# A fused two-block kernel: the layers' low halves on VectorE alone, the bias table loaded and masked later, head norms loaded once

## The chip, the cores and the metric

The kernel runs on one NeuronCore of a Trainium2 chip. Its engines are TensorE (PE), VectorE (DVE), ScalarE (ACT), GpSimd (POOL) and SyncE (SP), which only issues loads here. The metric is the device time of one execution in microseconds, as the median of several runs. Lower is better.

## The reference

The input is 256 tokens of width 1024 in float32. A first block (adaptive norm, two attentions, a mixture of 32 experts) is followed by a second block of two layers. Only the second block's layers are touched by the change. Cut to what matters:

```python
def second_block(x, ...):
    for l in range(DEPTH_2):                                  # 2 layers
        h = rmsnorm(x, norm_mix_pre[l])
        proj = jnp.einsum('bsd,de->bse', h, w_in[l])          # 1024 -> 5888
        qa, ka, va, pu, qc, kc, vc, gl = jnp.split(proj, splits, axis=-1)
        ya = global_axial_attention(qa, ka, va, qk_norm_q[l], qk_norm_k[l])
        yb = pool_mixer(pu, w_pool[l], pool_scale[l])
        yc = neighbourhood_attention(qc, kc, vc, rpb[l])
        ...                                                   # gates, branches, w_out
        x = x + rmsnorm(mix, norm_mix_post[l])
        h = rmsnorm(x, norm_ffn_pre[l])
        f = conv_gated_mlp(h, w_up[l], conv_w[l], conv_b[l], w_down[l])
        x = x + rmsnorm(f, norm_ffn_post[l])
    return x

def global_axial_attention(q, k, v, gq, gk):
    q = rmsnorm(q.reshape(B, S, A_HEADS, HEAD_DIM), gq)       # 8 heads of 64, one gain row gq
    k = rmsnorm(k.reshape(B, S, A_KV_HEADS, HEAD_DIM), gk)    # 2 heads
    q = rope_2d(q, row, col) * (HEAD_DIM ** -0.5)
    k = rope_2d(k, row, col)
    ...                                                       # softmax(q k) v

def neighbourhood_attention(q, k, v, rpb):
    ...                                                       # keys of a 16 column window
    bias = rpb[:, dr[None, :, None], dc[:, None, :]]          # s + bias, softmax, times v
```

## The kernel before

**Units and halves.** In a layer the weights come in 66 units of 1 MB (128 partitions x 2048 float32), which SP loads in a fixed order into a ring of three slots (`RING_L`). The first 23 units are `w_in`: 0 and 1 give q of attention a, 2 gives its k and v, 3 and 4 the pooling input, 5 and 6 q of attention c, 7 to 10 its k and v, 11 to 22 the gates. A product with such a unit is made in three passes of TensorE over rounded halves: ScalarE copies the unit to a rounded high half (`take_high`, L1730), then the low half, unit minus high half, is made, and TensorE multiplies high by high, low by high and high by low (L739, 48 matmuls a unit). There are two pairs of halves, so the high half of unit u waits until TensorE is done with unit u - 2. SP loads unit u when the low half of unit u - 3 is made.

**Who makes the low halves.** VectorE does it in `take_low` (L1417) with one subtraction 128x2048, for all units but 5, 6, 7 and 8, which `POOL_LOW` gives to GpSimd (L1918). `low_half_done` tells waiting engines which semaphore counts for a unit, `low_done` or `low_done_pool`.

**The start of a layer.** VectorE normalises x, TensorE turns it, then units 0 to 6 (`EARLY` = 7) are multiplied. Pooling products follow (L1048 and after), then transposes of the rotated q and k (L1062, L1067), scores of attention a, units 7 to 10, its values, scores of attention c, units 11 to 22. VectorE's order is written out by hand: low halves 1 to 4, then norm and rotation of q and k (L1448 to L1478), which ends in `rope_ready`, then the scores' evacuation with row maximum (`keep_scores`, L1132), the scaling by the sum (`normalise`, L1146), low halves 9 to 12 and the scores of c, for which `bias_masked` must be there.

**GpSimd's part of a layer.** It waits for x (`layer_in`), issues six loads on its own queue (L1908, L1909): the head norm of q, repeated for 8 heads, and of k, for 2 heads (into `gqk`), the pooling weights, the two post norm rows (into `gpost2`, all on 128 partitions), and the bias table of attention c (`tables`, 2 MB, from `neighbours`). When the table is in, it adds the window mask in one operation of 4096 columns (L1913) and sets `bias_masked`. Then it makes its four low halves, and much later the gated products of the MLP (L1925 to L1927).

## Time and profile before

| | us |
|---|---|
| median of 3 runs | 2227.37 |
| lowest, highest | 2223.24, 2229.26 |
| the profiled execution, its own time | 2221.66 |
| its span in the trace | 2220.0 |
| TensorE busy | 2024.0 (91%) |
| VectorE busy | 817.1 |
| ScalarE busy | 706.2 |
| GpSimd busy | 296.8 |
| first layer of the second block, from its first weight load | 1263.6 |
| second layer, first load of GpSimd's | 1741.6 |

The profile is of one execution. The chain of work that ended last is followed back from the last instruction, at each step to what released it; a piece named "issue" is time in which the engine waited for nothing that the profile shows, and a piece of a line is the part of that instruction that lies on the chain. In the timeline a row is a start, a duration, the engine, the line, what is written from what is read, and in brackets how long the engine stood idle before it and what ended that. Ends of matmuls are modelled: neighbouring ones overlap by 0.1 to 0.2 us in the rows. q1 is the queue of SP's loads, q0 that of GpSimd's; both run on the same 16 DMA engines.

### The profile page before, as it was taken

To read this page: it belongs to the slowest core of one execution; us is meant where nothing else is said; L and a number is where in the kernel's file an instruction comes from. 1 tells how busy PE (TensorE), PEld (TensorE's weight loads), DVE (VectorE), ACT (ScalarE), POOL (GpSimd) and SP (SyncE) were. 2 spreads that over 40 slices of the span, in tenths; PEclk is the share of its full clock that TensorE was granted. 3 is DMA by queue.
4 is the path that set the end of the run, shared out by engine and by line. 5 is a ranking of instruction groups with operands and counts; after the bars stand their busy time and mean duration, and the time that the engine had idled before them with its cause. 6 is when DMAs were issued, how large, how long until landed. Compare 5 with 4: busy or idle time off the path is not lost.

```text
span 2220.0 us, 30251 instructions
## 1 busy us (share of the span) xinstructions
PE 2024.0 (91%) x11629; PEld 1316.4 (59%) x11630; DVE 817.1 (37%) x1341; ACT 706.2 (32%) x1092; POOL 296.8 (13%) x221
## 2 busy tenths in 40 slices
PE   5998699999999999999999689997999679997998
PEld 2785333333333333333333278986998679987996
DVE  2443411211111111112111266425775475245763
ACT  2434111111111111111111335514553346415553
POOL 3040100000000010001000131000341140000440
PEclk7899699999999999999999889998999889998999
DMA  9776699998996999799999864434555733443553
GB/s 355 153 279 265 258 416 418 418 417 344 398 418 283 418 418 417 316 418 417 417 416 417 297 183 130 149 117 152 171 190 171 180 117 118 149 171 129 181 184 114
DMA packets 203889, 609.45 MB, mean 275 GB/s; under 512 B 10946, under 2 KB 115542, under 8 KB 167408
## 3 DMA queue, kind: packets, MB, share of 16 engines
q1 hardware_dynamic: 197600, 585.40, 68.8%
q0 software_dynamic: 5872, 21.87, 4.4%
q8 instruction: 61, 1.00, 0.2%
q10 hardware_dynamic: 328, 0.95, 0.1%
q14 instruction: 28, 0.23, 0.0%
HBM read 605.03 MB, written 9.24 MB: 277 GB/s over the span
## 4 chain that ended last, share of the span: by engine, by line
PE 66%; DMA 12%; DVE 7%; issue 6%; SPq 5%; ACT 4%; DVEq 0%; ACTq 0%
PE bank L739 29%; PE bank L996 15%; PE bank L1025 9%; DMA ring<-in_w_gate_up 7%; DMA ring<-in_w_in 4%; PE bank L1089 3%; PE bank L956 2%; SPq L620 2%; SPq L623 2%; DVE split L1417 1%; ACT probs L1572 1%; PE bank L969 1%; PE bank L989 1%; DMA ring<-in_w_ada 1%; ACT split L1730 1%
## 5 line engine op out<-in xcount | busy, mean ns | idle before, releaser
L996 PE MATMUL bank<-ring,qkv 128*64 128x512 f32 x2240 | 497.3, 597 | 13.6 <-DMA ring<-in_w_gate_up 13.6
L739 PE MATMUL bank<-hT_hi,split 128*128 128x256 f32 x2432 | 442.0, 285 | 7.2 <-DVE hT_lo L1425 4.0
L739 PEld LDWEIGHTS bank<-hT_hi,split 128*128 128x128 f32 x2432 | 381.5, 193 | 10.4 <-issue 6.4
L1417 DVE TENSOR_TENSOR split<-ring,split 128x2048 fp32r<-128x2048 f32 x112 | 275.0, 2456 | 262.5 <-ACT split L1730 262.5
L1730 ACT ACTIVATE split<-ring 128x2048 fp32r<-128x2048 f32 x120 | 229.6, 1913 | 422.7 <-PE bank L739 318.9
L996 PEld LDWEIGHTS bank<-ring,qkv 128*64 128x64 f32 x2240 | 155.4, 137 | 338.5 <-issue 294.2
L739 PE MATMUL bank<-hT_lo,split 128*128 128x256 f32 x1216 | 345.3, 284 | 0.0
L1025 PE MATMUL bank<-ring,qkv 128*64 128x512 f32 x1120 | 255.8, 598 | 25.7 <-ACT qkv L1691 22.7
L739 PEld LDWEIGHTS bank<-hT_lo,split 128*128 128x128 f32 x1216 | 234.7, 193 | 0.0
L1395 DVE SCALAR_TENSOR_TENSOR out_halves<-bank,probs,out_halves 64x512 fp32r<-64x512 f32 x70 | 52.5, 750 | 395.5 <-ACT out_halves L1713 395.0
L1385 DVE TENSOR_SCALAR qkv<-bank 128x512 f32<-128x512 f32 x35 | 24.2, 692 | 421.2 <-PE bank L996 421.2
L1701 ACT ACTIVATE qkv<-qkv 128x512 f32<-128x512 f32 x35 | 22.1, 631 | 482.0 <-DVE qkv L1385 482.0
L1025 PEld LDWEIGHTS bank<-ring,qkv 128*64 128x64 f32 x1120 | 85.2, 136 | 148.8 <-issue 116.8
L1889 POOL TENSOR_TENSOR bias_halves<-qkv,small 4x512 fp32r<-4x512 f32 x32 | 41.4, 1294 | 906.1 <-DMA qkv<-in_b_gate_up 906.1
L739 PE MATMUL bank<-split,hT_hi 128*128 128x256 f32 (+1 forms) x576 | 131.2, 323 | 22.2 <-DVE split L1417 17.9
L739 PEld LDWEIGHTS bank<-split,hT_hi 128*128 128x128 f32 x576 | 101.9, 206 | 29.7 <-DVE split L1417 19.7
L1925 POOL TENSOR_TENSOR gated_hi<-probs 128x512 fp32r<-128x512 f32 x22 | 40.8, 1853 | 583.7 <-ACT probs L1801 583.7
L739 PE MATMUL bank<-split,gated_hi 128*128 128x512 f32 x352 | 109.3, 390 | 2.0 <-DVE split L1417 2.0
L739 PE MATMUL bank<-split,hT_lo 128*128 128x256 f32 (+1 forms) x288 | 92.5, 321 | 0.0
L1695 ACT ACTIVATE qkv<-bank 128x512 f32<-128x512 f32 x36 | 21.5, 597 | 215.2 <-PE bank L962 215.2
L1089 PE MATMUL bank<-mixT,ring 128*128 128x256 f32 x384 | 83.4, 380 | 1.5 <-ACT mixT L1564 1.5
L1089 PEld LDWEIGHTS bank<-mixT,ring 128*128 128x128 f32 x384 | 72.8, 190 | 12.2 <-issue 2.4
(282 smaller groups left out, 2375.8 us busy)
## 6 DMA issues: line engine op xcount, KB each, us to landing
ring<-in_w_gate_up SPq DMA_DIRECT2D x256, 1024.0 KB, 16.9
ring<-in_w_down SPq DMA_DIRECT2D x150, 1024.0 KB, 15.6
ring<-in_w_in SPq DMA_DIRECT2D x58, 1024.0 KB, 5.5
ring<-in_w_up SPq DMA_DIRECT2D x44, 1024.0 KB, 5.1
ring<-in_w_ada SPq DMA_DIRECT2D x24, 1024.0 KB, 9.8
ring<-in_w_out SPq DMA_DIRECT2D x12, 1024.0 KB, 4.9
ring<-in_w_branch SPq DMA_DIRECT2D x12, 1024.0 KB, 5.1
neighbours<-rpb_copies POOLq DMA_DIRECT2D x32, 128.0 KB, 9.3
```

Source lines behind the costliest of these rows:

```text
L620: sp.dma_start(unit_at(u), wgu[:, u, :]).then_inc(landed_moe[u], 16)
L623: sp.dma_start(rows_unit(u), wdn[:, 2 * v:2 * v + 2, :]).then_inc(landed_moe[u], 16)
L739: last = pe.matmul(out, a[a_half], b[b_half], start=start and i == 0, stop=stop and i == 2)
L956: last = pe.matmul(rows_bank[CAP * j:CAP * j + CAP, :], sel[:, tt, :], htok[:, tt, 512 * j:512 * j + 512], start=(tt == 0), stop=(tt == TT ...
L996: last = pe.matmul(hidden[q][CAP * j:CAP * j + CAP, :], xgT[:, k % 4, k // 4, :], unit_at(k)[:, c:c + 512], start=False, stop=(k == KC - 1))
L1025: last = pe.matmul(rows_bank[CAP * half:CAP * half + CAP, :], actT[:, f % 4, f // 4, :], rows_unit(KC + v)[:, c, 512 * half:512 * half + 5 ...
L1089: last = pe.matmul(bs[i][:, c * T:c * T + T], wv[:, k, n0:n0 + P], mixT[:, 4 * (u // 2) + k, :], start=(k == 0), stop=(k == 3))
L1395: last = dve.scalar_tensor_tensor(out=y_halves[there, half, :], in0=banks[6][here, :], scalar=slot_gate[here, :], in1=y_halves[here, half, ...
L1417: dve.tensor_tensor(low, unit_at(u % RING_L), high.bitcast(F32), ALU.subtract).then_inc(low_done, 1)
L1730: act.activation(split_halves(u)[0], unit_at(u % RING_L), ACT.Copy).then_inc(high_done, 1)
L1889: pool.tensor_tensor(bias_halves[0].rearrange("r (a t) -> r a t", t=T), brows.rearrange("r (a t) -> r a t", t=T), zeros[96:100, :].unsquee ...
L1925: own(pool.tensor_tensor(high, value, gate, ALU.mult))
```

## The change

The change has four edits, all in the layers' loop.

- `POOL_LOW` and its semaphore go. VectorE makes all low halves; those of units 5 to 8 are put at three places of its order: 5 behind the mean squares of q and k, 6 behind the product with the head norms, 7 and 8 behind `rope_ready`.
- The head norms are loaded once for all heads: `gqk` has 2 x 64 columns in place of 640, and the product with it is two operations that read the row once for each head, in place of one.
- GpSimd issues the loads of the table and then of the two post norm rows only when TensorE is done with the seventh unit. The post norms have a semaphore of their own, `gpost_in`, for which VectorE waits before the first post norm.
- The mask is added in sixteen operations of 256 columns, one for each token tile and head.

```diff
-PARAMS_IN = 5
+PARAMS_IN = 3
+GPOST_IN = 2
...
-POOL_LOW = [5, 6, 7, 8]
-DVE_LOW = [u for u in SPLIT if u not in POOL_LOW]
...
-        gqk = scratch(8448, 640)
+        gqk = scratch(8448, 2 * DH).rearrange("p (i d) -> p i d", i=2)
...
-            mine, done = (POOL_LOW, low_done_pool) if u in POOL_LOW else (DVE_LOW, low_done)
-            return done, l * len(mine) + (mine.index(u) + 1)
+            return low_done, l * len(SPLIT) + (SPLIT.index(u) + 1)
...
                     .then_inc(qk_means, 1)
+                take_low(5)
                 dve.wait_ge(roots, seen(roots))
...
-                own(dve.tensor_tensor(qk, qk, gqk.unsqueeze(1).broadcast_to([P, TT, n_heads * DH]), ALU.mult))
+                for i, (a, n) in enumerate(((0, HEADS), (MIX, A_KV))):
+                    part = qk[:, :, a:a + n * DH].rearrange("p t (h d) -> p t h d", d=DH)
+                    last = dve.tensor_tensor(part, part, gqk[:, i, :].unsqueeze(1).unsqueeze(1).broadcast_to(
+                        [P, TT, n, DH]), ALU.mult)
+                own(last)
+                take_low(6)
...
                 last.then_inc(rope_ready, 1)
+                take_low(7, 8)
                 keep_scores("a", lambda tt, h: zeros)
...
+                dve.wait_ge(gpost_in, 16 * GPOST_IN * (l + 1))
                 post_norm([f"mix{j}" for j in range(4)], gpost2[0], x_mid)
...
-                loads = [(gqk[:, 0:MIX].rearrange("p (h d) -> p h d", d=DH), over_heads(qk_q, HEADS)),
-                         (gqk[:, MIX:].rearrange("p (h d) -> p h d", d=DH), over_heads(qk_k, A_KV)),
-                         (wpool, w_pool[one].rearrange("l g c d -> (l c) g d")),
-                         (gpost2[0], norm_mix_post[one].rearrange("l d -> (l d)").partition_broadcast(P)),
-                         (gpost2[1], norm_ffn_post[one].rearrange("l d -> (l d)").partition_broadcast(P))]
+                loads = [(gqk[:, 0, :], qk_q[one].rearrange("l d -> (l d)").partition_broadcast(P)),
+                         (gqk[:, 1, :], qk_k[one].rearrange("l d -> (l d)").partition_broadcast(P)),
+                         (wpool, w_pool[one].rearrange("l g c d -> (l c) g d"))]
...
+                pool.wait_ge(unit_done_l, l * N_UNITS + (RING_L + EARLY))
+                posts = [(gpost2[0], norm_mix_post[one].rearrange("l d -> (l d)").partition_broadcast(P)),
+                         (gpost2[1], norm_ffn_post[one].rearrange("l d -> (l d)").partition_broadcast(P))]
                 pool.dma_start(tables.rearrange("p t h k -> p (t h k)"),
                                neighbours[one].rearrange("l p t h k -> (l p) (t h k)")).then_inc(bias_l_in, 16)
+                for to, source in posts:
+                    pool.dma_start(to, source).then_inc(gpost_in, 16)
                 pool.wait_ge(bias_l_in, 16 * (l + 1))
-                groups = tables.rearrange("p t h (r c) -> p (t h r) c", c=GRID_W)
-                pool.tensor_tensor(groups, groups, const("window").unsqueeze(1).broadcast_to(
-                    [P, TT * HEADS * GRID_H, GRID_W]), ALU.add).then_inc(bias_masked, 1)
-                for u in POOL_LOW:
-                    pool.wait_ge(high_done, l * len(SPLIT) + (SPLIT.index(u) + 1))
-                    high, low = split_halves(u)
-                    pool.tensor_tensor(low, unit_at(u % RING_L), high.bitcast(F32), ALU.subtract).then_inc(low_done_pool, 1)
+                for tt in range(TT):
+                    for h in range(HEADS):
+                        piece = tables[:, tt, h, :].rearrange("p (r c) -> p r c", c=GRID_W)
+                        last = pool.tensor_tensor(piece, piece, const("window").unsqueeze(1).broadcast_to(
+                            [P, GRID_H, GRID_W]), ALU.add)
+                last.then_inc(bias_masked, 1)
```

VectorE between the projection of k and v and the first scores, in program order, before (L1417 is a low half; those of the units 2 to 4 stand ahead, the norm and rotation behind):

```order
L1417 TENSOR_TENSOR split<-ring,split 128x2048 [waits high_done]
L1448 TENSOR_TENSOR ring<-qkv 128x1280 [waits bank_free_l6]
L1449 TENSOR_REDUCE qkms<-ring 128x20 [waits dve_own]
L1452 RECIPROCAL qkr<-qkms 128x20 [waits roots]
L1455 TENSOR_TENSOR qkv<-qkv,qkr 128x1280 [waits dve_own]
L1457 TENSOR_TENSOR qkv<-qkv,ring 128x1280 [waits params_in]
L1465 TENSOR_TENSOR probs<-qkv,consts 128x640 [waits dve_own]
L1474 TENSOR_TENSOR qkv<-probs 128x2x512 [waits dve_own]
L1478 TENSOR_TENSOR probs<-probs 128x2x64 x4
```

The same place of the changed kernel, where the low half is L1416:

```order
L1447 TENSOR_TENSOR ring<-qkv 128x1280 [waits bank_free_l6]
L1448 TENSOR_REDUCE qkms<-ring 128x20 [waits dve_own]
L1416 TENSOR_TENSOR split<-ring,split 128x2048 [waits high_done]
L1452 RECIPROCAL qkr<-qkms 128x20 [waits roots]
L1459 TENSOR_TENSOR qkv<-qkv,ring 128x2x512 [waits params_in]
L1459 TENSOR_TENSOR qkv<-qkv,ring 128x2x128
L1416 TENSOR_TENSOR split<-ring,split 128x2048 [waits high_done]
L1470 TENSOR_TENSOR probs<-qkv,consts 128x640
L1483 TENSOR_TENSOR probs<-probs 128x2x64 x4
L1416 TENSOR_TENSOR split<-ring,split 128x2048 [waits high_done]
L1416 TENSOR_TENSOR split<-ring,split 128x2048 [waits high_done]
```

Low halves 5 and 6 now stand inside norm and rotation, 7 and 8 between it and the scores.

GpSimd from the start of a layer to the gated products, before:

```order
L1908 ISA [waits layer_in]
L1908 DMA ring<-in_qk_norm_q 128x8x64
L1908 DMA ring<-in_qk_norm_k 128x2x64
L1908 DMA ring<-in_w_pool 128x4x128
L1908 DMA side<-in_norm_mix_post 128x1024
L1908 DMA side<-in_norm_ffn_post 128x1024
L1909 DMA ring<-neighbours 128x4096
L1913 TENSOR_TENSOR ring<-ring,consts 128x4096 [waits bias_l_in]
L1918 TENSOR_TENSOR split<-ring,split 128x2048 [waits high_done]
L1925 TENSOR_TENSOR gated_hi<-probs 128x512 [waits gelu_ready]
```

And in the changed kernel:

```order
L1910 ISA [waits layer_in]
L1910 DMA ring<-in_qk_norm_q 128x64
L1910 DMA ring<-in_qk_norm_k 128x64
L1910 DMA ring<-in_w_pool 128x4x128
L1916 ISA [waits unit_done_l]
L1916 DMA ring<-neighbours 128x4096
L1919 DMA side<-in_norm_mix_post 128x1024
L1919 DMA side<-in_norm_ffn_post 128x1024
L1924 TENSOR_TENSOR ring<-ring,consts 128x256 [waits bias_l_in]
L1924 TENSOR_TENSOR ring<-ring,consts 128x256 x15
L1933 TENSOR_TENSOR gated_hi<-probs 128x512 [waits gelu_ready]
```

The table and the post norms moved behind the wait for `unit_done_l`, the table ahead of them, and the four low halves (L1918, of which one row stands above) are gone.

## Rows read from the trace of the kernel before

**Rows 1.** The page: busy time of each engine, share of the span, instructions.

```profile
PE 2024.0 (91%) x11629; PEld 1316.4 (59%) x11630; DVE 817.1 (37%) x1341; ACT 706.2 (32%) x1092; POOL 296.8 (13%) x221
```

**Rows 2.** A window over the first layer's start: stretch, length, busy engines, PEclk, DMA, GB/s.

```profile
1264.00:1344.00 80.00, 56.12 (x379) 53.99 (x379) 55.23 (x43) 32.29 (x48) 34.94 (x11) 0.83 0.71 192
```

**Rows 3.** The chain that ended last, first layer: start, length on the chain, what.

```profile
1283.94 21.30 DMA ring<-in_w_in
...
1307.89 6.22 issue
1314.10 5.86 DVE ring L1448
```

**Rows 4.** The same chain, start of the second layer.

```profile
1745.75 26.89 DMA ring<-in_w_in
...
1774.68 7.16 DVE split L1417
...
1798.40 5.70 DVE qkv L1457
```

**Rows 5.** Timeline of ScalarE: high halves that TensorE released.

```profile
1335.83 1.91 ACT L1730 ACTIVATE split<-ring 128x2048 fp32r<-128x2048 f32 x1 [5.00 <-PE bank L739]
...
1417.42 1.91 ACT L1730 ACTIVATE split<-ring 128x2048 fp32r<-128x2048 f32 x1 [3.12 <-PE bank L739]
...
1423.18 1.91 ACT L1730 ACTIVATE split<-ring 128x2048 fp32r<-128x2048 f32 x1 [3.12 <-PE bank L739]
```

**Rows 6.** Timeline of TensorE: its idle times in both layers' starts.

```profile
1302.26 0.39 PE L739 MATMUL bank<-split,hT_hi 128*128 128x256 f32 x1 [2.35 <-DVE split L1417]
...
1314.23 0.58 PE L739 MATMUL bank<-split,hT_hi 128*128 128x256 f32 x1 [4.45 <-DVE split L1417]
...
1343.61 1.97 PE L1062 MATMUL bank<-consts,qkv 128*128 128x128 f32 x8 [2.63 <-DVE probs L1478]
...
1781.88 0.58 PE L739 MATMUL bank<-split,hT_hi 128*128 128x256 f32 x1 [9.62 <-DVE split L1417]
...
1818.14 1.97 PE L1062 MATMUL bank<-consts,qkv 128*128 128x128 f32 x8 [4.14 <-DVE probs L1478]
```

**Rows 7.** DMA queue q0 in 1276:1282 and 1298:1300: packets, MB, share of engines.

```profile
q0 software_dynamic: 32, 0.13, 105.8%
...
q0 software_dynamic: 27, 0.41, 48.4%
```

**Rows 8.** Timeline of GpSimd: mask, two low halves, a product of 512 columns.

```profile
1303.06 8.96 POOL L1913 TENSOR_TENSOR ring<-ring,consts 128x4096 f32<-128x4096 f32 x1 [27.45 <-DMA ring<-neighbours]
...
1324.67 5.05 POOL L1918 TENSOR_TENSOR split<-ring,split 128x2048 fp32r<-128x2048 f32 x1 [6.07 <-ACT split L1730]
...
1570.27 1.30 POOL L1926 TENSOR_TENSOR probs<-probs 128x512 f32<-128x512 f32 x1
...
1792.32 4.59 POOL L1918 TENSOR_TENSOR split<-ring,split 128x2048 fp32r<-128x2048 f32 x1 [12.64 <-ACT split L1730]
```

**Rows 9.** Timeline of VectorE: low half, rotation, reciprocal, normalisations, scores of c.

```profile
1299.91 2.29 DVE L1417 TENSOR_TENSOR split<-ring,split 128x2048 fp32r<-128x2048 f32 x1 [7.24 <-ACT split L1730]
...
1325.31 5.09 DVE L1465 TENSOR_TENSOR probs<-qkv,consts 128x640 f32<-128x640 f32 x1
...
1335.55 0.81 DVE L1465 TENSOR_TENSOR probs<-qkv,consts 128x640 f32<-128x640 f32 x1
...
1355.38 2.19 DVE L1146 TENSOR_SCALAR probs<-probs,small 128x256 f32<-128x256 f32 x8
...
1359.33 2.19 DVE L1146 TENSOR_SCALAR probs<-probs,small 128x256 f32<-128x256 f32 x8
1361.44 2.28 DVE L1417 TENSOR_TENSOR split<-ring,split 128x2048 fp32r<-128x2048 f32 x1
...
1383.80 0.42 DVE L1132 CUSTOM_DVE_ANT_0 probs<-bank,ring 128x256 f32<-128x256 f32 x1 [3.96 <-issue]
...
1792.95 0.28 DVE L1452 RECIPROCAL qkr<-qkms 128x20 f32<-128x20 f32 x1 [6.00 <-ACT qkms L1758]
```

More of the change, by code:

```diff
@@ L486, in build @@
         landed_l = [sem(f"landed_l{s}") for s in range(RING_L)]
-        high_done, low_done, low_done_pool, hT_high = (sem(n) for n in ("high_done", "low_done", "low_done_pool", "hT_high"))
+        high_done, low_done, hT_high = (sem(n) for n in ("high_done", "low_done", "hT_high"))
         unit_done, tile_done = sem("unit_done"), sem("tile_done")
@@ L504, in build @@
         y_ready, moe_done = sem("y_ready"), sem("moe_done")
-        layer_in, params_in, bias_l_in, bias_masked = sem("layer_in"), sem("params_in"), sem("bias_l_in"), sem("bias_masked")
+        layer_in, params_in, gpost_in = sem("layer_in"), sem("params_in"), sem("gpost_in")
+        bias_l_in, bias_masked = sem("bias_l_in"), sem("bias_masked")
         qk_means, rope_ready, branch_ready, gated_ready = sem("qk_means"), sem("rope_ready"), sem("branch_ready"), sem("gated_ready")
@@ L1896, in _ @@
                 pool.wait_ge(layer_in, TT * l + TT)
-                def over_heads(a, n):
-                    return a[one].rearrange("l d -> (l d)").unsqueeze(0).broadcast_to([n, DH]).partition_broadcast(P)
-                loads = [(gqk[:, 0:MIX].rearrange("p (h d) -> p h d", d=DH), over_heads(qk_q, HEADS)),
-                         (gqk[:, MIX:].rearrange("p (h d) -> p h d", d=DH), over_heads(qk_k, A_KV)),
-                         (wpool, w_pool[one].rearrange("l g c d -> (l c) g d")),
-                         (gpost2[0], norm_mix_post[one].rearrange("l d -> (l d)").partition_broadcast(P)),
-                         (gpost2[1], norm_ffn_post[one].rearrange("l d -> (l d)").partition_broadcast(P))]
+                loads = [(gqk[:, 0, :], qk_q[one].rearrange("l d -> (l d)").partition_broadcast(P)),
+                         (gqk[:, 1, :], qk_k[one].rearrange("l d -> (l d)").partition_broadcast(P)),
+                         (wpool, w_pool[one].rearrange("l g c d -> (l c) g d"))]
                 assert len(loads) == PARAMS_IN
@@ L1908, in _ @@
                     pool.dma_start(to, source).then_inc(params_in, 16)
+                pool.wait_ge(unit_done_l, l * N_UNITS + (RING_L + EARLY))
+                posts = [(gpost2[0], norm_mix_post[one].rearrange("l d -> (l d)").partition_broadcast(P)),
+                         (gpost2[1], norm_ffn_post[one].rearrange("l d -> (l d)").partition_broadcast(P))]
+                assert len(posts) == GPOST_IN
                 pool.dma_start(tables.rearrange("p t h k -> p (t h k)"),
                                neighbours[one].rearrange("l p t h k -> (l p) (t h k)")).then_inc(bias_l_in, 16)
+                for to, source in posts:
+                    pool.dma_start(to, source).then_inc(gpost_in, 16)
                 pool.wait_ge(bias_l_in, 16 * (l + 1))
-                groups = tables.rearrange("p t h (r c) -> p (t h r) c", c=GRID_W)
-                pool.tensor_tensor(groups, groups, const("window").unsqueeze(1).broadcast_to(
-                    [P, TT * HEADS * GRID_H, GRID_W]), ALU.add).then_inc(bias_masked, 1)
-                for u in POOL_LOW:
-                    pool.wait_ge(high_done, l * len(SPLIT) + (SPLIT.index(u) + 1))
-                    high, low = split_halves(u)
-                    pool.tensor_tensor(low, unit_at(u % RING_L), high.bitcast(F32), ALU.subtract).then_inc(low_done_pool, 1)
+                for tt in range(TT):
[4 more added lines that the diff above has]
+                last.then_inc(bias_masked, 1)
                 own.loop(l, 2 * UPAIRS)
```

## The prediction, made before the changed kernel ran

> **What bounds the kernel now.** I first looked for the stage that the diff touches, since the mean over the span says little: TensorE is busy 91% of it and GpSimd 13% [rows 1]. The code that changes is the start of the two layers of the second block, at about 1263 us and 1735 us, up to the first attention. There I read the chain that ended last. It should run through matmuls if TensorE were the bound. It doesn't: in the first layer it runs through a weight load that takes 21.30 us to land, then through VectorE operations that last about 4.4 us too long [rows 3]; in the second through a load of 26.89 us and VectorE operations of 7.16 and 5.70 us [rows 4].
>
> Then I looked at TensorE's own timeline for what this costs. In a steady stretch one weight unit takes 5.76 us (ScalarE's high halves of two neighbouring units start at 1417.42 and 1423.18, each ending its wait for TensorE) [rows 5]. In the first layer TensorE idles 2.35 and 4.45 us between units and 2.63 us before the transposes of q and k; in the second 9.62 us in one piece and 4.14 us before the transposes [rows 6]. The clock falls with such gaps too: its mean granted share in this stretch of the first layer is 0.83 [rows 2].
>
> Why is the load late? GpSimd's queue q0 moved 32 packets, 0.13 MB, in the 6 us from 1276 and held the 16 engines 105.8% of that time: 6 x 16 x 1.058 / 32 = 3.2 us for a 4 KB packet. Behind the head norms, two microseconds of the table's stretch moved 27 packets with 0.41 MB at 48.4%, 0.57 us each, most of 16 KB [rows 7]. The slow packets are made of 256 byte pieces, the head norm repeated for each head. The two head norm loads are 128 x (8 + 2) x 256 bytes = 320 KB, 80 packets, 80 x 3.2 / 16 = 16 us in which all 16 engines do little else. Weight units share those engines.
>
> Why are the VectorE operations long? A low half alone takes 2.29 us, and the first rotary product 0.81, but 5.09 when GpSimd's low half of 5.05 us, begun at 1324.67, runs [rows 8, 9]: 5.09 - 0.81 = 4.3 us. It ended when GpSimd's did (1329.7). A SBUF operation of two tensors waits there for the whole GpSimd instruction. The square of q and k (5.86 against 1.5 us) and two later rotary operations show the same, and the low half at 1307 waited for the mask's end at 1312.0 [rows 3, 8].
>
> **Part 1, head norms once.** Now 2 x 128 x 256 bytes = 64 KB, 16 packets, 16 x 3.2 / 16 = 3.2 us of the engines instead of 16. The loads of the two post norms (1 MB) and the table (2 MB) leave this stretch too. The fourth and fifth unit then land within a few us of their issue; they are needed only when TensorE is done with the unit two before, 10 us or more later. The load's stall is gone. What is late next is the halves: a high half may start when the unit two before is done, 1.91 us on ScalarE and 2.29 on VectorE, with handovers 4.35 us against a pitch of 5.76. There is 1.25 us of slack a unit, so TensorE should run unit after unit.
>
> First layer: unit 2 ended at 1302.26 - 2.35 = 1299.9 [rows 6]. Four units at 5.76 end at 1322.9 (before: 1335.8, when the high half of unit 8 was released [rows 5]). The pooling products follow; before they took 1335.8 to 1343.61 - 2.63 = 1341.0, 5.2 us. The transposes could start at 1328.1 instead of 1343.6: **15.5 us**. Second layer: unit 2 ended at 1781.88 - 9.62 = 1772.3, four units to 1795.3, 5.2 us to 1800.5, against 1818.14: **17.6 us**.
>
> **Part 2, low halves 5 to 8 on VectorE.** VectorE gets 4 x 2.29 = 9.2 us a layer, GpSimd loses 4 x 4.6 or more. Two of the four stand ahead of the rotated q and k. Can VectorE hold the date 1328.1? Its stretch from the square at 1314.10 [rows 3] to the release of the transposes at 1343.6 [rows 6] is 29.5 us; four operations in it wait some 4.4 us each for GpSimd, 17.5 together, so 12 us are work. With two low halves that is 12 + 4.6 = 16.6 us, and it begins when low half 4 is done, 1299.9 + 4.3 = 1304.2. It ends at 1320.8 if neither waits for ScalarE: high half 5 is ready at 1307.6 (the mean squares end at 1307.3), high half 6 at 1313.4 (the norm products end at 1313.4). So 1321, 7 us ahead of 1328. Low halves 5 and 6 end at 1309.9 and 1315.8, their units start at 1311.3 and 1317.0, slack 1.2 to 1.4 us. Low half 8 ends near 1327.3, the first scores come near 1332. I cost this part at nothing; its cover is the slack of 1.2 us, and each us beyond it costs one. The gain of no longer waiting for GpSimd is inside the 15.5 and 17.6 already. The head norm product is split in two, 1024 and 256 columns for 1280: one instruction's fixed time more, under 0.2 us, inside the 7 us.
>
> **Part 3, the late table.** GpSimd waits for the seventh unit, 1322.9. Behind this wait stand the table's load, the post norms', the mask and, much later, the gated products. The table is first in the queue. At some 0.6 us for 16 KB its 128 packets take 5 us alone, up to 10 beside the weight units issued at 1323 and 1327. With 2 us from wait to first packet it lands at 1330 to 1335; before it took 27.45 us of waiting [rows 8], behind the head norms. The post norms are wanted 100 us later. The weight units of this stretch are wanted after 1348, so they can lose 5 us.
>
> The mask: 4096 columns in 8.96 us, 2048 in 4.6 [rows 8], so about 2.1 ns a column and 0.25 us an instruction; a piece of 256 columns is 0.8 us, sixteen 13 us. Between 0.56 (8.96 / 16) and 1.3 a piece (what 512 columns take) are the bounds, 9 to 21 us. The mask ends at 1345, at the latest 1335 + 21 = 1356. Scores of attention c want it at 1383.8 - 15.5 = 1368.3 [rows 9]. Hidden, with 12 us to spare at worst.
>
> **What the pieces collide with.** The mask now runs beside attention a. Its VectorE chain is scores, then two normalisations of eight operations, 2.19 us each, then low half 9, which unit 9 waits for within half a microsecond [rows 9]. Moved by 15.5 these are at 1339.9, 1343.8 and 1345.9. With the mask at 1332 to 1345, 5 us of pieces are left when the first normalisation starts. Does a one-input operation in SBUF wait for GpSimd? Rows give both: the rotary product waits, but a reciprocal of 20 columns takes its 0.28 us at 1792.95 in the middle of GpSimd's low half [rows 8, 9]. Bounds: nothing, or all that is left of the mask less the 1.5 us of slack between the normalisations: (1345 - 1339.9) - 1.5 = 3.6, from 1.5 to 6.5 with the table's landing. I take 3 us a layer, nearer the rotary product, since the normalisation is as large as a piece and the reciprocal is tiny.
>
> The Trainium skill bears on this choice (SBUF — State Buffer, section "SBUF: two separate sides"): VectorE and GpSimd lock one shared port pair for a whole instruction, VectorE when it has two SBUF inputs or runs in a two-port fast mode. For the two-input case the trace agrees (4.3 us of waiting at 1325.31). The normalisation, one input and fp32 in SBUF, would be in the fast mode by that page; by it the sum has the 3 us, without it 0. No row here shows a normalisation beside GpSimd.
>
> **The sum.** 15.5 + 17.6 - 2 x 3 = 27 us. The profiled execution took 2221.66 us, its span 2220.0; it would become 2194.6. The median shown is 5.7 us above it, within the spread of the three runs (2223.24 to 2229.26), so against the median: 2227.4 - 27 = **2200**. No later stage gives it back, as far as I see: from unit 7 on both layers run the same steps at the same distances, paced by TensorE.
>
> **Rivals.**
> *No collision at the normalisation*: the table lands early or one-input operations don't wait. 2227.4 - 33 = 2194. For it speaks the reciprocal. The page above speaks against it.
> *The pieces cost more*: pieces of 1.3 us, or the score operations wait too. 21 us of mask from 1332, of which 8 hold VectorE: 33 - 16 = 17, so 2210.
> *Low halves late*: the 1.2 us of slack is not there (ScalarE copies in between), and three units wait 1 to 1.5 us in each layer: 27 - 8 = 19, so 2208.
> *The slow packets stay*: the head norm loads cost their 16 us for another reason than their size, say a single source row. Then the late loads remain, 9.6 + 2.5 us in the second layer and some 8 in the first are lost again: 27 - 20 = 7, so 2220, the same within what can be told.
> *Slower*: the sixteen pieces each hold one VectorE operation of attention a for the whole piece, with no slack. At 1.3 us that is 21 us a layer, 42 in all against 33: 2236. It decides from 33.1 / 32 = 1.03 us a piece, with all sixteen on VectorE's path. Against it: the mask has begun before the normalisations, and between the score and exponential steps VectorE has idle time.
>
> **How the numbers follow.** Forecast 2200: 0.48. No collision, 2194: 0.26. Pieces cost more, 2210: 0.10. Low halves late, 2208: 0.07. Slow packets stay, 2220: 0.05. Slower, 2236: 0.04. The first four reach from 2194 - 4 to 2210 + 2, with the spread of the median at each end: range 2189 to 2212, which leaves out the last two and the tails. A measurement of this kernel tells 0.3%, 6.7 us, from no change. Faster by more: 0.92; within: 0.04; slower: 0.04.
>
> **What would show it.** In the changed profile TensorE's idle time between units 2 and 6 is gone in both layers, and the fifth unit's load lands in under 10 us. The rotary operations last 0.8 and not 5 us. The transposes start some 28 us after unit 2's end and don't wait for VectorE. The mask is sixteen pieces of 0.8 us that start 8 to 12 us after the seventh unit. If normalisations next to them last 0.7 to 1 us an operation, unit 9 starts 3 us late; if they don't, the time is 2194. I am wrong if a load between 1273 and 1300 still takes over 15 us, if units 5 and 6 wait for VectorE's low halves, or if attention c waits for the mask.

## The result, and the profile after

The changed kernel takes 2197.76 us (median of 4 runs, 2195.05 to 2200.45) against 2228.32 us of the kernel before in the same comparison (2223.24 to 2232.04). The ratio is 0.9871, 95% interval 0.9849 to 0.9893, so 24 to 34 us fewer. The profiled execution of after has a span of 2197.5 us. Other executions of the kernel before, taken beside the experiments, had medians of 2224 to 2226 us, so differences of a few microseconds are read from distances within a trace and not from the medians.

The page of after, busy time of each engine, to be held against [rows 1]:

```profile
PE 2017.9 (92%) x11629; PEld 1311.4 (60%) x11630; DVE 800.1 (36%) x1351; ACT 704.7 (32%) x1092; POOL 260.6 (12%) x243
```

VectorE has ten instructions more, 1351 for 1341, among them eight low halves of 2.3 us that GpSimd made before. Yet it is busy 17 us less. A row's duration holds the time in which an instruction waits for GpSimd's (5.09 us for 0.81 in [rows 9]), and such waits went.

The chain that ended last, first layer (start, length on the chain, what), for [rows 3]:

```profile
1267.25 5.39 DMA ring<-in_w_in
...
1284.53 42.08 PE bank L738 x336
```

All seven units are one piece of 336 matmuls, 7 x 48, with no load and no VectorE between them. That is a stage at TensorE's own pace. The mean granted clock went from 0.83 [rows 2] to 0.88 over a window that covers the same work:

```profile
1264.00:1334.00 70.00, 53.34 (x394) 51.67 (x394) 43.66 (x50) 36.23 (x56) 3.51 (x6) 0.88 0.59 188
```

TensorE's timeline of after, for [rows 6]: start, duration, instruction, and in brackets the idle time and what ended it.

```profile
1284.53 0.38 PE L738 MATMUL bank<-split,hT_hi 128*128 128x256 f32 x1 [2.17 <-DVE hT_lo L1424]
...
1331.61 1.04 PE L1061 MATMUL bank<-consts,qkv 128*128 128x128 f32 x8
1332.48 0.60 PE L1066 MATMUL bank<-consts,probs 128*128 128x128 f32 x4
...
1338.59 0.50 PE L738 MATMUL bank<-hT_hi,split 128*128 128x256 f32 x2 [0.26 <-DVE small L1131]
...
1353.20 0.39 PE L738 MATMUL bank<-split,hT_hi 128*128 128x256 f32 x1 [2.84 <-DVE split L1416]
...
1813.87 0.39 PE L738 MATMUL bank<-split,hT_hi 128*128 128x256 f32 x1 [2.87 <-DVE split L1416]
```

The gaps of 2.35, 4.45 and 9.62 us between units, and those of 2.63 and 4.14 us ahead of the transposes, are gone. A new one stands ahead of unit 9 in both layers, 2.84 and 2.87 us. Where it comes from is seen on the two engines that share it, GpSimd first, then VectorE:

```profile
1337.37 11.59 POOL L1924 TENSOR_TENSOR ring<-ring,consts 128x256 f32<-128x256 f32 x16 [8.49 <-DMA ring<-neighbours]
```

```profile
1319.33 0.82 DVE L1470 TENSOR_TENSOR probs<-qkv,consts 128x640 f32<-128x640 f32 x1
...
1337.61 0.50 DVE L1135 TENSOR_SCALAR small<-small 128x8 f32<-128x8 f32 x1
...
1340.96 0.64 DVE L1135 TENSOR_SCALAR small<-small 128x8 f32<-128x8 f32 x1
...
1342.48 5.89 DVE L1145 TENSOR_SCALAR probs<-probs,small 128x256 f32<-128x256 f32 x8
1348.28 0.19 DVE L1142 RECIPROCAL small<-small 128x8 f32<-128x8 f32 x1
1348.51 2.44 DVE L1145 TENSOR_SCALAR probs<-probs,small 128x256 f32<-128x256 f32 x8
1350.87 2.28 DVE L1416 TENSOR_TENSOR split<-ring,split 128x2048 fp32r<-128x2048 f32 x1
```

The first rotary product takes 0.82 us in place of 5.09 [rows 9]. The sixteen mask pieces run from 1337.4 to 1349.0. The first normalisation lies inside and takes 5.89 us for 2.19 [rows 9], the second 2.44. Low half 9 starts 2.4 us late by that, and unit 9 waits for it.

**Distances that noise touches least.** From the start of unit 0 to that of unit 7, and from unit 7 to unit 11, in us, first and second layer, worked out from the starts of the units in each trace:

| kernel | 0 to 7 | 7 to 11 | median, its own before |
|---|---|---|---|
| before | 70.7, 72.8 | 36.1, 36.1 | |
| after | 54.1, 54.1 | 39.8, 39.8 | 2197.8, 2228.3 |
| head norms once, alone (e1) | 68.4, 61.9 | 35.6, 36.1 | 2209.8, 2224.9 |
| low halves on VectorE, alone (e10) | 66.4, 64.1 | 35.9, 35.9 | 2209.2, 2224.3 |
| after, norms repeated (e2) | 54.1, 54.1 | 39.7, 39.8 | 2199.1, 2224.9 |
| after, low halves on GpSimd (e3) | 62.5, 61.9 | 36.4, 39.7 | 2209.9, 2224.9 |
| after, one mask piece (e4) | 54.1, 55.2 | 36.0, 36.0 | 2187.5, 2224.9 |
| after, one mask operation (e6) | 62.3, 62.1 | 36.5, 37.8 | 2207.5, 2224.3 |
| after, mask later (e5) | 53.9, 53.7 | 35.9, 35.9 | 2187.3, 2224.3 |
| the same, loads early (e9) | 53.8, 53.8 | 35.9, 35.9 | 2190.3, 2224.3 |
| one mask operation, later (e8) | 53.8, 54.8 | 35.9, 35.9 | 2190.3, 2226.2 |
| after, ten distinct rows (e7) | 54.1, 54.9 | 39.7, 39.8 | 2197.4 (one run), 2226.2 |
| after, norms in ten loads (e11) | 52.7, 53.9 | 39.5, 39.8 | 2195.8 (one run), 2226.2 |

Where one of these kernels is 1 us off after's 54.1 (55.2 of e4, 54.8 of e8, 54.9 of e7, 52.7 of e11), the difference lies in unit 0, which takes 8.3 to 8.4 us or 5.9 for 7.3.

After against before: 16.6 + 18.7 us gained up to unit 7, 3.7 + 3.7 given back up to unit 11, 27.9 in all. The rest of the 22.5 us by which the two profiled spans differ lies outside these distances: the first layer of after begins 3.6 us later (1284.53 against 1280.89), in code that neither kernel changed. This isn't one odd execution: in the traces of after and of the nine kernels built on it unit 0 starts at 1283.2 to 1287.2, in those of before, e1 and e10 at 1280.4 to 1280.9. Why, no run tells.

### The profile page after: what moved, and what is told of

It is laid out like the page before. It is cut to its first block, busy times and chain, and to the rows that moved or that the text cites. A ratio compares the mean times of both kernels' runs of the same rounds, so it can differ in the third digit from the quotient of the medians.

```text
span 2197.5 us, 30287 instructions
## 1 busy us (share of the span) xinstructions
PE 2017.9 (92%) x11629; PEld 1311.4 (60%) x11630; DVE 800.1 (36%) x1351; ACT 704.7 (32%) x1092; POOL 260.6 (12%) x243
## 4 chain that ended last, share of the span: by engine, by line
PE 70%; DMA 10%; SPq 5%; issue 5%; DVE 5%; ACT 3%; DVEq 0%; ACTq 0%
PE bank L738 33%; PE bank L995 15%; PE bank L1024 9%; DMA ring<-in_w_gate_up 7%; PE bank L1088 3%; PE bank L955 2%; SPq L619 2%; SPq L622 2%; DMA ring<-in_w_in 2%; PE bank L968 1%; PE bank L988 1%; DMA ring<-in_w_ada 1%; ACT probs L1579 1%; DVE split L1416 1%; PE bank L788 1%
## 5 line engine op out<-in xcount | busy, mean ns | idle before, releaser
L1416 DVE TENSOR_TENSOR split<-ring,split 128x2048 fp32r<-128x2048 f32 x120 | 283.8, 2367 | 265.1 <-ACT split L1737 264.9
L1088 PEld LDWEIGHTS bank<-mixT,ring 128*128 128x128 f32 x384 | 72.8, 190 | 12.2 <-issue 2.4
## 6 DMA issues: line engine op xcount, KB each, us to landing
ring<-in_w_ada SPq DMA_DIRECT2D x24, 1024.0 KB, 10.1
```

Source lines behind the costliest of these rows:

```text
L1088: last = pe.matmul(bs[i][:, c * T:c * T + T], wv[:, k, n0:n0 + P], mixT[:, 4 * (u // 2) + k, :], start=(k == 0), stop=(k == 3))
L1416: dve.tensor_tensor(low, unit_at(u % RING_L), high.bitcast(F32), ALU.subtract).then_inc(low_done, 1)
```

## The experiments

My theory at this point: two causes in the kernel before, late loads and GpSimd holding VectorE, and one new cost, the mask beside the normalisations. The rivals are that one of the causes is everything, or that the late loads come from the 3 MB and not from the head norms.

### e1: the head norms once, alone

```diff
-        gqk = scratch(8448, 640)
+        gqk = scratch(8448, 2 * DH).rearrange("p (i d) -> p i d", i=2)
...
-                loads = [(gqk[:, 0:MIX].rearrange("p (h d) -> p h d", d=DH), over_heads(qk_q, HEADS)),
+                loads = [(gqk[:, 0, :], qk_q[one].rearrange("l d -> (l d)").partition_broadcast(P)),
...
```

The load of k's norm and the product in two operations are changed as in the change itself.

> The kernel before, with one edit: the head norms are loaded once for all heads, and the product with them is two operations. Table, post norms, one mask operation and GpSimd's four low halves stay where they were. My theory (two causes that add: slow head norm packets that hold up weight units, and GpSimd instructions that hold up VectorE): the 21.3 and 26.9 us loads fall below 12 us and TensorE's 4.45 and 9.62 us gaps go, but the table now lands near 1290 and its 9 us mask holds low half 2 or 3, and the rotation still loses 4.4 us at each of four places. Gain 14 to 20 us, 2208 to 2214. Rival A, the loads are everything: the full 30 us, 2198. Rival B, the late loads came from the 3 MB of table and post norms, not from the head norms: the gaps stay, gain under 6 us, above 2222.

Measured 2209.77 us, ratio 0.9937 (0.9912 to 0.9962): 15 us gained, as expected. GpSimd's timeline in this kernel, then VectorE's and TensorE's:

```profile
1287.45 9.00 POOL L1917 TENSOR_TENSOR ring<-ring,consts 128x4096 f32<-128x4096 f32 x1 [12.38 <-DMA ring<-neighbours]
```

```profile
1290.76 10.05 DVE L1417 TENSOR_TENSOR split<-ring,split 128x2048 fp32r<-128x2048 f32 x2 [7.52 <-ACT split L1734]
...
1314.92 5.00 DVE L1455 TENSOR_TENSOR qkv<-qkv,qkr 128x1280 f32<-128x1280 f32 x1
```

```profile
1298.67 0.38 PE L739 MATMUL bank<-split,hT_hi 128*128 128x256 f32 x1 [4.14 <-DVE split L1417]
```

The table arrives 12.4 us after its issue in place of 27.5 [rows 8], the late units are gone, and just by that the 9 us mask begins at 1287.45 and holds two low halves, 10.05 us for what alone takes 4.6. In the first layer that gives back nearly all (0 to 7: 70.7 to 68.4). In the second the mask falls between two low halves and holds the later one by 0.9 us only (72.8 to 61.9). The rotation still waits for GpSimd.

### e10: low halves 5 to 8 on VectorE, alone

```diff
-POOL_LOW = [5, 6, 7, 8]
+POOL_LOW = []
...
+                take_low(5)
...
+                take_low(6)
...
+                take_low(7, 8)
```

> The kernel before, with one edit: VectorE makes low halves 5 to 8 at the three new places. Loads, table and mask as before. The late loads of 21 and 27 us stay, so the gaps of 4.5 and 9.6 us stay; the rotation no longer waits for GpSimd. Gain: the wait ahead of the transposes, 2.6 and 4.1 us, and 1 us per layer of late units: 2216 to 2219. Rival: the rotation was the bound, and gaps upstream are made up by it, gain 15 us or more, 2210.

Measured 2209.16 us, ratio 0.9937 (0.9912 to 0.9961): 15 us, by distances 4.3 + 8.7 = 13.0 up to unit 7. I expected 5 to 8, and my rival's 2210 is what came, though not by its mechanism, since the gaps upstream are still there:

```profile
1302.96 0.39 PE L739 MATMUL bank<-split,hT_hi 128*128 128x256 f32 x1 [3.42 <-DVE split L1417]
...
1315.23 0.58 PE L739 MATMUL bank<-split,hT_hi 128*128 128x256 f32 x1 [4.78 <-DVE split L1417]
...
1342.73 4.36 PE L789 MATMUL bank<-qkv 64*128 64x256 f32 x32 [0.88 <-ACT qkv L1567]
```

One term that I had left out lies at the transposes. With no idle time ahead of them they run at full clock: twelve take 1.5 us in after (1331.61 to 1333.08, above) and in this kernel, where before they took from 1343.61 to 1346.43, 2.8 us. The windows over them, first before, then after (stretch, length, busy engines, PEclk, DMA, GB/s), show a granted clock of 0.50 behind the idle 2.63 us of [rows 6], and of 1.00 without it:

```profile
1343.60:1346.50 2.90, 2.82 (x12) 2.42 (x12) 0.00 (x0) 1.23 (x3) 0.00 (x0) 0.50 0.76 236
```

```profile
1331.60:1333.10 1.50, 1.48 (x13) 1.23 (x11) 0.00 (x0) 1.50 (x4) 0.00 (x0) 1.00 0.88 369
```

The load of the second layer came 1.7 us less late as well (gap 7.94 for 9.62), which I can't attribute.

### e2: after, with the head norms repeated again

> The changed kernel with the head norm edit alone undone: both head norms are loaded repeated for 8 and 2 heads again, and the product is one operation. If the slow packets alone cause the late units, TensorE's gap of 4.5 to 10 us is back in each layer: 2208 to 2218. If they matter only together with the table and the post norms behind them: head norms and pooling weights take 80 x 3.2 + 64 x 0.7 = 301 us of the 16 engines, 19 us from 1273, the fourth and fifth unit land at 1290 to 1297, before they are wanted at 1294 and 1300, and it costs 0 to 3 us: 2198 to 2201. I expect the second.

The edit is e1's, in reverse, on the changed kernel. Measured 2199.12 us, ratio 0.9878 (0.9848 to 0.9909), and the distances of after to 0.1 us. Loading the head norms once is worth nothing once the table and the post norms have moved. One weight unit still takes 21.6 us to land in the first layer. It lands at 1299.2, and TensorE starts it without a gap at 1304.1. The next one, unit 4, is where the two causes add. Counted from the start of unit 0 it lands after 24.3 us in before, 16.9 here, 9.0 in e9 (single norms, early table) and 8.2 in after.

The late load isn't all of the gaps of 4.45 and 9.62 us either. In before the low half behind it then waits for the mask operation, until 1312.0 in the first layer, 4.5 us too long, and takes 7.16 us for 2.3 in the second [rows 3, 4, 8]. So all of the first gap and 4.9 us of the second are the mask's, and the mask too has moved in after.

### e3: after, with the low halves on GpSimd

```diff
+                for u in POOL_LOW:
+                    pool.wait_ge(high_done, l * len(SPLIT) + (SPLIT.index(u) + 1))
+                    high, low = split_halves(u)
+                    pool.tensor_tensor(low, unit_at(u % RING_L), high.bitcast(F32), ALU.subtract).then_inc(low_done_pool, 1)
                 pool.wait_ge(unit_done_l, l * N_UNITS + (RING_L + EARLY))
```

> The changed kernel with the four low halves of units 5 to 8 back on GpSimd, ahead of its wait for the seventh unit. My theory: GpSimd's low half takes 4.6 us against 2.3, so units 5 and 6 start 1 to 2 us late, and the rotation loses 4.4 us at three or four places, 13 to 17 us, against 7 us of slack and 4.6 us of low halves that VectorE no longer does: 4 to 6 us a layer, 2206 to 2210 in all. Rival: the slack hides it, 2198 to 2200.

Measured 2209.85 us, ratio 0.994 (0.9918 to 0.9961), inside my range, but with 8.4 and 7.8 us more up to unit 7 where I expected 4 to 6 a layer. VectorE's timeline has the held operations back:

```profile
1311.65 5.00 DVE L1457 TENSOR_TENSOR qkv<-qkv,qkr 128x1280 f32<-128x1280 f32 x1
1316.78 5.76 DVE L1461 TENSOR_TENSOR qkv<-qkv,ring 128x1024 f32<-128x1024 f32 x2
...
1323.32 5.30 DVE L1477 TENSOR_TENSOR probs<-qkv,consts 128x320 f32<-128x320 f32 x2
...
1329.28 5.22 DVE L1477 TENSOR_TENSOR probs<-qkv,consts 128x320 f32<-128x320 f32 x2
```

Four waits of about 4 us. Of the edits that were undone one at a time on after (e2, e3, e6), this one costs the most, 12 us by the medians.

### e4: after, with one mask piece

```diff
-                for tt in range(TT):
-                    for h in range(HEADS):
+                for tt in range(TT - 1, TT):
+                    for h in range(HEADS - 1, HEADS):
```

> The changed kernel with one mask piece in place of sixteen (attention c then sees unmasked keys in the other heads, so this leaves work out). If the 2.8 us gap before unit 9 and the slow clock behind it come from the pieces beside the normalisations, both are gone: the distance from unit 7 to unit 11 falls from 39.8 back to 36.1 us in each layer, 7.5 us in all, 2190 to 2191. Rival, the gap comes from something else in the new order (low halves 7 and 8 on VectorE, later loads): it stays, 2197 to 2198.

Measured 2187.48 us, ratio 0.9832 (0.9807 to 0.9858). That is 2.5 us under my range, but unit 7 to unit 11 takes 36.0 us in both layers, as expected. TensorE's wait ahead of unit 9:

```profile
1350.91 0.39 PE L738 MATMUL bank<-split,hT_hi 128*128 128x256 f32 x1 [0.51 <-DVE split L1416]
```

0.51 us in place of 2.84, and unit 9 itself takes 5.9 in place of 7.3 us from its start to that of unit 10. The windows over it, first in after, then here, show why: granted clock 0.77 behind the gap, 1.00 without it.

```profile
1353.20:1360.50 7.30, 7.30 (x48) 7.30 (x49) 2.15 (x1) 0.00 (x0) 0.00 (x0) 0.77 0.85 270
```

```profile
1350.90:1356.80 5.90, 5.89 (x49) 5.89 (x50) 2.29 (x1) 1.93 (x2) 0.00 (x0) 1.00 0.74 204
```

The first normalisation, 5.89 us in after, has its 2.19 us again:

```profile
1342.52 2.19 DVE L1145 TENSOR_SCALAR probs<-probs,small 128x256 f32<-128x256 f32 x8
```

So the collision costs 3.8 us a layer, 2.3 of waiting and 1.5 of clock.

### e6: after, with the mask as one operation

```diff
-                for tt in range(TT):
-                    for h in range(HEADS):
...
+                groups = tables.rearrange("p t h (r c) -> p (t h r) c", c=GRID_W)
+                pool.tensor_tensor(groups, groups, const("window").unsqueeze(1).broadcast_to(
+                    [P, TT * HEADS * GRID_H, GRID_W]), ALU.add).then_inc(bias_masked, 1)
```

> The changed kernel with the mask as one operation of 4096 columns at the same place. One instruction from 1337.4 would end at 1346.3 and hold the first normalisation until then; that one would end at 1348.4, the second at 1350.9, low half 9 at 1353.2, just where the pieces put it (GpSimd ends 2.6 us earlier for lack of fifteen fixed times, VectorE is held in one piece). So the same within 1.5 us: 2196 to 2199. Rival, small pieces are what makes the late mask bearable: unit 9 starts 4 us or more later than with pieces, 2205 or above.

Measured 2207.47 us, ratio 0.9925 (0.99 to 0.995): my expectation was wrong and the rival right. GpSimd, VectorE and TensorE in this kernel:

```profile
1337.17 8.80 POOL L1922 TENSOR_TENSOR ring<-ring,consts 128x4096 f32<-128x4096 f32 x1 [8.65 <-DMA ring<-neighbours]
```

```profile
1337.26 8.74 DVE L1135 TENSOR_SCALAR small<-small 128x8 f32<-128x8 f32 x1
```

```profile
1346.48 0.79 PE L738 MATMUL bank<-hT_hi,split 128*128 128x256 f32 x2 [8.50 <-DVE small L1131]
```

The first operation that meets the mask isn't a normalisation. It is the change of sign of eight row maxima (L1135, 0.17 us alone), between the first and the second eight scores. It waits 8.6 us for the mask's end. The second eight scores stay in their banks behind it, and unit 7 waits for those banks. In after the same operation meets pieces and takes 0.50 and 0.64 us. So the sixteen pieces are worth 8.2 us a layer up to unit 7, less 2.0 to 3.3 us that they lose after it, and not by being shorter in sum (11.6 against 8.8 us), but because no wait is longer than a piece.

### e5, e9 and e8: the mask behind low half 10

```diff
                 pool.wait_ge(bias_l_in, 16 * (l + 1))
+                pool.wait_ge(low_done, l * len(SPLIT) + (SPLIT.index(10) + 1))
                 for tt in range(TT):
```

> The changed kernel with one more wait: GpSimd starts the sixteen mask pieces when low half 10 is done, so they stand between the normalisations of attention a and the scores of c. If only the collision at the normalisations costs, the gap before unit 9 goes as it did without the mask, and the mask ends some 8 us ahead of the scores of c: unit 7 to unit 11 takes 36 us, 2188 to 2191. Rival: the pieces then hold low halves 11 and 12 or come late for the scores, and it stays at 2197.

Measured 2187.27 us, ratio 0.9835 (0.9807 to 0.9862), the lowest median here (not told apart from e4, e8 and e9 within the spread), with all of the work in it. The two distances are 53.9 and 35.9 us. GpSimd's mask and VectorE's low halves 11 and 12, which it meets:

```profile
1355.36 15.21 POOL L1925 TENSOR_TENSOR ring<-ring,consts 128x256 f32<-128x256 f32 x16 [25.61 <-DVE split L1416]
```

```profile
1359.43 2.30 DVE L1416 TENSOR_TENSOR split<-ring,split 128x2048 fp32r<-128x2048 f32 x1 [4.15 <-ACT split L1737]
1365.19 2.74 DVE L1416 TENSOR_TENSOR split<-ring,split 128x2048 fp32r<-128x2048 f32 x1 [3.46 <-ACT split L1737]
```

Here GpSimd is the one that waits (15.2 us for 11.6). It ends at 1370.6, 0.9 us ahead of the first score of c (1371.45) and not the 8 us that I expected: the place is just wide enough for sixteen pieces.

> As the kernel with the later mask, but table and post norms are loaded at the layer's start again, ahead of no wait; the head norms are loaded once. GpSimd's queue then needs 16 x 3.2 + 64 x 0.7 + 256 x 0.17 + 128 x 0.6 = 217 us of the 16 engines, 13.5 us, and units 3 and 4 land by 1290 and 1295 before they are wanted at 1298 and 1303.5. If a late unit needs both the slow head norms and the 3 MB, TensorE runs without a gap and the time equals the later mask's: 2188 to 2192. If the moved load was needed by itself, a gap of 3 us or more returns between units 2 and 4: 2196 or above.

The edit is the wait for the seventh unit taken out of e5. Measured 2190.3 us, ratio 0.9841 (0.9816 to 0.9866), and distances of 53.8 and 35.9 us. So the later load isn't needed either, if the head norms are loaded once and the mask has a place of its own (in e1, without one, an early table meant an early mask).

> The kernel with the later mask, but as one operation of 4096 columns behind low half 10. It would run from about 1355 to 1364 and hold low half 11, due near 1358.5, until 1364, done 1366.3; unit 11 comes near 1375, behind the scores of c. So nothing that TensorE waits for is late: 2187 to 2190, as with sixteen pieces. Rival: an instruction that long beside VectorE always costs, as it did at the earlier place, 2195 or above.

Measured 2190.26 us, ratio 0.9838 (0.9797 to 0.9878). GpSimd, then VectorE:

```profile
1355.57 9.05 POOL L1923 TENSOR_TENSOR ring<-ring,consts 128x4096 f32<-128x4096 f32 x1 [25.60 <-DVE split L1416]
```

```profile
1359.64 9.33 DVE L1416 TENSOR_TENSOR split<-ring,split 128x2048 fp32r<-128x2048 f32 x2 [4.16 <-ACT split L1737]
```

One operation of 9.05 us at this place holds low half 11 and makes 12 follow late, and nobody wants them before it ends. Pieces are worth their cost only where someone waits.

### e7 and e11: what makes the head norm packets slow

In the kernel before q0 held the engines 105.8% of 6 us for 32 packets, 3.2 us each [rows 7]. The queue of the weight loads, q1, moved no packet at all in these 6 us, though the load of unit 3 had been issued at 1273.4; it landed at 1297.9. The prediction took the 256 byte pieces for the cause and hence 3.2 us for each packet left. The load queue of after in 1276:1282, with the head norms once and the pooling weights (packets, MB, share of the engines):

```profile
q0 software_dynamic: 144, 0.33, 19.5%
```

6 x 16 x 0.195 / 144 = 0.13 us a packet, as a mean over three kinds. By size, the 32 packets of 2 KB that the head norms take had 0.15 us each, though their pieces are 256 bytes as before; the 64 of the pooling weights have 4 KB, and 48 closing ones 4 bytes. Two kernels on the base of e2 tell more. The edit of e7 against e2, then that of e11:

```diff
-                loads = [(gqk[:, 0:MIX].rearrange("p (h d) -> p h d", d=DH), over_heads(qk_q, HEADS)),
-                         (gqk[:, MIX:].rearrange("p (h d) -> p h d", d=DH), over_heads(qk_k, A_KV)),
+                distinct = w_in2[one].rearrange("l (p k) n -> (l p) (k n)", p=P)[:, 0:2560].rearrange(
+                    "p (h d) -> p h d", d=4 * DH)[:, :, 0:DH]
+                loads = [(gqk[:, 0:MIX].rearrange("p (h d) -> p h d", d=DH), distinct[:, 0:HEADS, :]),
+                         (gqk[:, MIX:].rearrange("p (h d) -> p h d", d=DH), distinct[:, HEADS:HEADS + A_KV, :]),
```

```diff
+                loads = [*((gqk[:, DH * i:DH * i + DH], qk_q[one].rearrange("l d -> (l d)").partition_broadcast(P))
+                           for i in range(HEADS)),
...
```

> The kernel with the head norms repeated again, but the ten 256 byte pieces of each partition are read from distinct places of a weight matrix, so no two pieces share an address (the gains of q and k are then wrong numbers; this changes what is computed, not its shape). The q0 packets of 4 KB took 3.2 us with the repeated row; in the changed kernel the 32 packets of 2 KB of the single rows took 0.13 to 0.18 us each, though their pieces are 256 bytes as well. If the small piece were slow, these packets stay near 3 us. If reading one row again and again is what is slow, or the zero step form of the load, they fall to 0.2 to 0.7 us. I expect the second.

> The same 1280 pieces of 256 bytes from the same two rows as with the repeated head norms, but issued as ten loads, each one row to all partitions, in place of two loads with an inner repeat. If the repeated address itself is slow (a thousand reads of one row), the packets stay near 3 us per 4 KB. If only the inner zero step form is slow, they take about 0.15 us per 2 KB and the q0 stretch ends within 6 us. I expect fast packets, since the post norms' and the single rows' loads read one row 128 times and are not slow.

The queue in the same 6 us, first with distinct rows (e7), then with ten loads of the same two rows (e11):

```profile
q0 software_dynamic: 192, 0.59, 40.4%
```

```profile
q0 software_dynamic: 80, 0.10, 52.0%
```

With distinct rows all 0.59 MB pass at 6 x 16 x 0.404 / 192 = 0.20 us a packet (0.27 us for one of 4 KB). The piece's size is not the cause. With ten loads only 0.10 MB pass in this time, and the 160 packets of 2 KB that the head norms take there had 1.03 us each on average, and the last ends near 1296; here I expected fast packets and was wrong. So the inner zero step form isn't the cause either. What is left is that the same row is read again and again: q's row 1024 times and k's 256 times in before and in e11, each 128 times in after. That it takes a thousand reads isn't shown: in e11 seven of the first sixteen packets already take 0.9 to 1.6 us, the other nine 0.1. From which number of reads, or of reads at one time, it turns slow, and in which part of the memory path, no run here tells. Both kernels took the time of after (one run each, 2197.4 and 2195.8), as e2 did.

## Why the prediction was right, point by point

The forecast was 2200 us; the median is 2197.8, the profiled span 2197.5 where the sum led to some 2193 (2220.0 - 27).

- *The bound.* Right: neither TensorE nor a load by itself, but two kinds of wait that entered its chain, for a load and for GpSimd. Once they are gone the seven units are one piece of 42.08 us.
- *Part 1, head norms once, the late loads.* The consequence is right (the load stall is gone), the attribution was too simple. In these traces TensorE waits for a load only with both the repeated norms and the 3 MB behind them: without the 3 MB ahead of unit 7 the norms may be repeated (e2), with single norms the 3 MB may stay (e9). Of the gaps of 4.45 and 9.62 us, 4.5 and 4.9 were the mask holding the low half behind the load. The price of the remaining head norm packets, 3.2 us of the engines, was wrong by its step "256 byte pieces": it is 32 packets x 0.15 / 16 = 0.3 us. It was hidden, so the sum didn't feel it; that the wrong cause did no harm is luck.
- *The units at 5.76 us.* Right: unit 2 to unit 6 takes 4 x 5.76 us in both layers, with no gap. The slack of 1.2 us held; low half 5 started at 1311.30, low half 6 at 1317.12, with units 5 and 6 at 1314.9 and 1320.7.
- *15.5 and 17.6 us up to the transposes.* Measured 16.6 and 18.7 up to unit 7. The 1.1 us a layer are mainly the transposes at full clock (1.5 us for 2.8), which my sum had at the price of before. The e10 expectation missed the same term.
- *Part 2 at nothing.* Right in effect. Rotation ended at 1324.6, 7.0 us ahead of the transposes, for the 7 us of the prediction.
- *Part 3, the table.* The mask could start 10.1 us after the table's issue (1337.37 against 1327.24), inside my 7 to 12. Pieces take 0.76 us on average for the 0.8 estimated, and the mask 11.6 us for 13. Attention c didn't wait.
- *The collision, 3 us a layer.* Measured 3.8 with e4, within the bounds of 1.5 to 6.5. The direction of the unknown (does a one-input operation in SBUF wait?) is settled for the normalisation: 5.89 us for eight that take 2.19, and gone without the mask. What I took as waiting alone is 2.3 us of it; 1.5 us are unit 9 at the lower clock behind the gap.
- *The sum.* 16.6 + 18.7 - 7.4 = 27.9 for a predicted 27. Two misses offset each other, 2.2 us more gained up to unit 7 and 1.4 us more lost behind it. The rest of the match is partly luck: the medians differ by 30.6 us and the two profiled spans by 22.5, of which 3.6 are the later start that no run explains.

The Trainium skill (SBUF — State Buffer, section "SBUF: two separate sides") states the lock for operations with two SBUF inputs and for fast one-input operations. The runs agree with the first by the rotary products (5.09 us for 0.81 [rows 9], and those of e3), and with the second by the normalisation beside pieces (5.89 us for 2.19) and by the 128 x 8 change of sign that waits 8.6 us in e6. Reciprocals do not wait: 0.28 us for 128 x 20 inside GpSimd's low half [rows 9], 0.19 us for 128 x 8 among the pieces (1348.28, above).

The rival *no collision* is refuted by e4, *pieces cost more* and *low halves late* by the rows of after. The rival *the slow packets stay* had a true core: in ten loads of single rows they do stay slow (e11), but with the late table that is hidden (e2 and e11 take the time of after). For *slower* no row of after speaks; its mechanism, an instruction of attention a held in full by the mask, is what e6 shows at 8 us a layer.

## What to carry to other kernels

GpSimd work isn't free because GpSimd is idle: for each of its operations on SBUF, ask which VectorE operation runs beside it and who waits for that one, and include the tiny ones. Place it where VectorE's results are not wanted for its whole duration; then its length doesn't matter (e8), and where that place is missing, cut it in pieces (0.5 to 0.64 us for the first operation that meets it against 8.7, e6). A load that lands late can have two sufficient cures, so undo each alone before paying for both: here one wait more (e5) was worth 8 us by the distances, and of the two edits on loads either could have been left out (the second of them only where the mask keeps its late place, e9).

## What the runs showed of the hardware that I had not expected

- Reading two 256 byte rows of device memory 1280 times in all holds a DMA engine 3.2 us for 4 KB [rows 7]; with distinct rows it is 0.27 us for 4 KB (e7), and with 256 reads in all 0.15 us for 2 KB (after). Split over ten loads it stays slow, 1.03 us for 2 KB (e11).
- A one-input VectorE operation on 128 x 8 float32 waited 8.6 us for a GpSimd operation (8.74 us in place of 0.17, e6), while score operations that read PSUM, and reciprocals, ran beside the mask with their usual durations.
- An idle stretch of 2.8 us on TensorE cost 1.5 us more behind it: unit 9 took 7.3 us at a mean granted clock of 0.77, and 5.9 us at 1.00 without the gap (e4).
